# Sixteen dense tokens moved to the row path of a PEER layer, the V pass turned feature-major, and the last norm of the dense tokens with it

## The reference, cut to what matters

```python
q = (xt @ w_pq).reshape(T, PEER_HEADS, PEER_QUERY)
s1 = einsum('thd,nd->thn', q[..., :PEER_HALF], sub_keys1)
s2 = einsum('thd,nd->thn', q[..., PEER_HALF:], sub_keys2)
...                                   # top 16 of each, top 16 of their 256 sums
gate = softmax(top_s)                 # idx: (T, 8, 16) numbers of experts
u_sel = take(peer_u, ib, axis=0)
act = gelu(einsum('thkd,td->thk', u_sel, xb)) * gb
v_sel = take(peer_v, ib, axis=0)
out = einsum('thk,thkd->td', act, v_sel)
x = layer_norm(DN_ALPHA * x + out, ln3_g, ln3_b)
```

## Time and profile before

| | |
|---|---|
| median of 3 runs | 3217.24 us (3212.23 to 3222.93) |
| the profiled execution's own time | 3216.38 us |
| its span, first to last instruction | 3214.6 us |
| TensorE busy | 3086.2 us, 96% |
| VectorE busy | 2062.2 us, 64% |
| GpSimd / ScalarE busy | 656.9 us, 20% / 362.9 us, 11% |
| moved by DMA | 1029.74 MB, mean 320 GB/s |
| granted TensorE clock, mean | 0.986 |

### The profile page before, as it was taken

How to read it: one execution, slowest core, us unless ns; L and a number is a source line. 1 busy time by engine, 2 the same in 40 slices (tenths; PEclk the granted TensorE clock), 3 DMA queues, 4 the chain that set the end, 5 groups by cost and what they waited for, 6 DMA issues and landing times.

```text
span 3214.6 us, 26896 instructions
## 1 busy us (share of the span) xinstructions
PE 3086.2 (96%) x10342; PEld 1887.6 (59%) x10342; DVE 2062.2 (64%) x3070; ACT 362.9 (11%) x650; POOL 656.9 (20%) x551
## 2 busy tenths in 40 slices
PE   8999999999998998899988999999999999999797
PEld 5444444444446676679863447885448874478543
DVE  5365533433767788979996866655566565656684
ACT  1223212301002111112210000000000000000000
POOL 0000000000221133331223342222222222222340
PEclk9999999999999999999999999999999999999999
DMA  7222221077995699999989999999999999999994
GB/s 274 73 78 72 83 77 47 36 275 245 377 422 231 272 367 377 380 383 354 382 336 414 376 419 421 422 418 416 418 421 422 419 418 416 421 421 421 413 411 185
DMA packets 152520, 1029.74 MB, mean 320 GB/s; under 512 B 16464, under 2 KB 21712, under 8 KB 35664
## 3 DMA queue, kind: packets, MB, share of 16 engines
q0 software_dynamic: 78512, 557.88, 42.4%
q1 hardware_dynamic: 73888, 470.24, 37.5%
HBM read 1007.08 MB, written 20.97 MB: 320 GB/s over the span
## 4 chain that ended last, share of the span: by engine, by line
DMA 42%; PE 33%; DVE 19%; issue 4%; POOL 1%; ACT 1%; DVEq 0%; SPq 0%; ACTq 0%
DMA arena<-peer_v,arena 39%; PE ps L707 11%; DVE arena L1880 7%; PE ps L1143 5%; PE ps L1116 3%; PE ps L879 2%; PE ps L897 2%; DVE arena L1921 2%; DVE arena L1869 2%; PE ps L778 1%; DVE arena L1918 1%; DMA arena<-peer_ut 1%; DVE arena L1807 1%; PE ps L671 1%; PE ps L832 1%
## 5 line engine op out<-in xcount | busy, mean ns | idle before, releaser
L1143 PE MATMUL ps<-arena 128*128 128x512 f32 x2048 | 887.6, 596 | 38.7 <-DVE arena L1932 35.2
L1116 PE MATMUL ps<-arena 128*128 128x256 f32 x4096 | 893.9, 380 | 5.2 <-DMA arena<-peer_ut 4.6
L1116 PEld LDWEIGHTS ps<-arena 128*128 128x128 f32 x4096 | 776.2, 190 | 113.2 <-DMA arena<-peer_ut 5.7
L1880 DVE SCALAR_TENSOR_TENSOR arena<-arena 128x2048 f32<-128x2048 f32 x256 | 601.5, 2349 | 305.3 <-DMA arena<-peer_v,arena 234.7
L1869 DVE CUSTOM_DVE_ANT_0 arena<-arena 128x2048 f32<-128x2048 f32 x256 | 585.9, 2289 | 288.1 <-DMA arena<-peer_u,arena 287.2
L1143 PEld LDWEIGHTS ps<-arena 128*128 128x128 f32 x2048 | 391.4, 191 | 532.6 <-issue 488.6
L628 POOL DMA_INDIRECT arena<-peer_u,arena x256 | 326.8, 1277 | 1085.3 <-DVE arena L1869 909.1
L639 POOL DMA_INDIRECT arena<-peer_v,arena x256 | 307.9, 1203 | 756.6 <-DVE arena L1880 731.4
L707 PE MATMUL ps<-arena 128*128 128x512 f32 x800 | 345.2, 592 | 1.0 <-ACT arena L1183 1.0
L707 PEld LDWEIGHTS ps<-arena 128*128 128x128 f32 x800 | 152.0, 190 | 191.9 <-issue 191.9
L1183 ACT ACTIVATE arena<-ps 128x512 f32<-128x512 f32 (+2 forms) x247 | 144.2, 613 | 726.1 <-PE ps L889 136.7
(11 more groups left out here) (181 smaller groups left out, 1791.3 us busy)
## 6 DMA issues: line engine op xcount, KB each, us to landing
arena<-peer_ut SPq DMA_DIRECT2D x128, 1024.0 KB, 9.2
arena<-peer_vt SPq DMA_DIRECT2D x128, 1024.0 KB, 9.1
arena<-w_row SPq DMA_DIRECT2D x52, 1024.0 KB, 8.9
arena<-w_mix SPq DMA_DIRECT2D x48, 1024.0 KB, 5.8
arena<-w_once SPq DMA_DIRECT2D x74, 512.0 KB, 3.5
arena<-w_feat SPq DMA_DIRECT2D x20, 1024.0 KB, 9.6
dense_gates<-arena SPq DMA_DIRECT2D x8, 2048.0 KB, 8.5
arena<-dense_gates POOLq DMA_DIRECT2D x11, 1024.0 KB, 24.2
```

The costliest lines, as they stand in the source:

```text
L1116: last = pe.matmul(ps[:, (e // 2) % 4, (e % 2) * DT:(e % 2 + 1) * DT], w[:, kt * P:(kt + 1) * P], XTD[:, kt * DT:(kt + 1) * DT], start=(kt ...
L1143: last = pe.matmul(bank(4 + (c % 2) * 2 + tb), G[:, t * DT + tb * P:t * DT + (tb + 1) * P], w[:, i * 512:(i + 1) * 512], start=(t == 0), s ...
L1880: dve.scalar_tensor_tensor(out=acc, in0=VB[e], scalar=AV[r // 4 % 2][:, r % 4:r % 4 + 1], in1=acc, op0=ALU.mult, op1=ALU.add).then_inc(v_f ...
```

## The change

The first 240 of the 256 dense tokens stay dense (`DN` = 240). The last 16 (`NX`) go to the row path as a third set of rows: 16 tokens x 8 heads fill the 128 partitions, so 16 rows r are enough for them, against 128 for a full block (`QUADS` = 68 quads where there were 64). They stand at quads 60 to 63 (`XQUAD` = 60); the last four quads of block 1 move behind them. Their x is written to DRAM once per head and read back as one tile `XE` (over `SC`), their expert numbers and gates go the same way; ScalarE starts the accumulator `ACCE` at alpha x / 8, and at the end TensorE sums the eight heads with a stationary 128x16 matrix `SEL`.

U tiles now move 240 columns where they moved 256. In the V pass `peer_vt` is stationary (128 experts x 128 features) and `G` moves, 240 tokens; a tile is 16 matmuls; the output is feature-major in `YT`. There are eight column groups c of 256 features (`NC`), and c = 0 and 1 alternate tile by tile, so that each weigh still stands ahead of two tiles. The gates are made for 60 fours of tokens, stored in ten groups of 24. The statistics of the last norm of the dense tokens come from TensorE with a matrix of ones (`sums`), the norm is done on feature-major tiles by VectorE and ScalarE, and the host turns the output. The two gain tiles of the last norm are loaded later.

```diff
-ET = 4
+ET = 8
+NC = 8
+NX = 16
+DN = DT - NX
-TG = 32
+TG = 24
+NQ = DN // 4
+QUADS = RSTEPS + TOPK // 4
 def half_pos(k):
     n = k - HALVES_BEFORE
-    return 1 + n if n < 4 else 5 + (n - 4) * (POSITIONS - 8) // (2 * RSTEPS - HALVES_BEFORE - 4)
+    return 1 + n if n < 4 else 5 + (n - 4) * (POSITIONS - 8) // (2 * QUADS - HALVES_BEFORE - 4)
+XROWS_POS = POSITIONS - 2 * TILES[3] + 6
+XQUAD = min(j for j in range(QUADS) if half_pos(2 * j - 2) >= XROWS_POS)
+def v_order(g):
+    last = TILES[g] // ET
+    return [(c, l) for l in range(last) for c in (0, 1)] + [(c, l) for c in range(2, NC) for l in range(last)]
...
+            def store_extra():
+                sp.wait_ge(steps_dv, DVE_AT["d.x2_1"])
+                for h in range(PH):
+                    sp.dma_start(rows_d[:, h, :], X[P - NX:P, 3 * D:4 * D]).then_inc(extra_out, 16)
+                sp.wait_ge(extra_set, 1)
+                sp.dma_start(idx_d, S1D[P - NX:P, HK:2 * HK].bitcast(I32)).then_inc(extra_out, 16)
+                sp.wait_ge(gated, 12)
+                sp.dma_start(gate_d, GATE4[P - NX:P, 3 * HK:4 * HK]).then_inc(extra_out, 16)
...
+                if p == u3 + SLOTS:
+                    c, l = v_order(2)[-1]
+                    sp.wait_ge(wb_used, W_AT[f"V2.{c}.{l}"])
+                    sp.dma_start(XE, rows_d.rearrange("t h n -> (t h) n")).then_inc(xe_in, 16)
+                if p == u3 + TILES[3] + SLOTS + 6:
+                    sp.wait_ge(g_ready, NK // 8)
+                    sp.dma_start(GAIN3_G, gains[6:7, :].partition_broadcast(P)).then_inc(gain3_in, 16)
+                    sp.dma_start(GAIN3_B, gains[7:8, :].partition_broadcast(P)).then_inc(gain3_in, 16)
...
-                    last = pe.matmul(ps[:, (e // 2) % 4, (e % 2) * DT:(e % 2 + 1) * DT], w[:, kt * P:(kt + 1) * P],
-                                     XTD[:, kt * DT:(kt + 1) * DT], start=(kt == 0), stop=(kt == KT - 1))
+                    last = pe.matmul(ps[:, (e // 2) % 4, (e % 2) * DT:(e % 2) * DT + DN], w[:, kt * P:(kt + 1) * P],
+                                     XTD[:, kt * DT:kt * DT + DN], start=(kt == 0), stop=(kt == KT - 1))
...
-                    for i in range(4):
-                        t = 4 * l + i
-                        last = pe.matmul(bank(4 + (c % 2) * 2 + tb), G[:, t * DT + tb * P:t * DT + (tb + 1) * P],
-                                         w[:, i * 512:(i + 1) * 512], start=(t == 0), stop=(t == TILES[g] - 1))
+                for i in range(ET):
+                    t = ET * l + i
+                    for k in range(2):
+                        last = pe.matmul(ps[:, 4 + (c % 2) * 2 + k, 0:DN], w[:, (2 * i + k) * P:(2 * i + k + 1) * P],
+                                         G[:, t * DN:(t + 1) * DN], start=(t == 0), stop=(t == TILES[g] - 1))
+            def sums(c):
+                pe.wait_ge(sq_ready, c + 1)
+                for k in range(2):
+                    f = 2 * c + k
+                    pe.matmul(ps[:, 0, 0:DN], ONES, YT[:, f * DN:(f + 1) * DN], start=(f == 0), stop=(f == KT - 1))
+                    last = pe.matmul(ps[:, 1, 0:DN], ONES, SQ3[c % 2][:, k * DN:(k + 1) * DN],
+                                     start=(f == 0), stop=(f == KT - 1))
+                last.then_inc(sums_mm, 1)
+            def extra_heads(half):
...
+                for k in range(2):
+                    q = 2 * half + k
+                    pe.matmul(ps[0:NX, 2 + k, :], SEL, ACCE[:, q * 512:(q + 1) * 512], start=True, stop=True
+                              ).then_inc(extra_mm, 1)
...
             def dot(r):
-                b = r // HK
-                dve.tensor_tensor_reduce(UB[e], UB[e], xrow(b), 1.0, 0.0, ALU.mult, ALU.add,
+                if r == 4 * XQUAD:
+                    dve.wait_ge(xe_in, 16)
+                xr = XE if is_extra(r // 4) else xrow(main_quad(r // 4) // (HK // 4))
+                dve.tensor_tensor_reduce(UB[e], UB[e], xr, 1.0, 0.0, ALU.mult, ALU.add,
...
+                    if g == 3 and (c, l) == (6, 0):
+                        dve.wait_ge(extra_ev, 4)
+                        norm(XE, XE, GAIN3_G, GAIN3_B, dve_tick).then_inc(y_ready, 1)
...
+            dve.wait_ge(sums_mm, NC)
+            link(dve.tensor_scalar(MU3, ps[:, 0, 0:DN], 1.0 / D, None, ALU.mult))
...
+            rsqrt(RSTD3, VAR3, NEWTON3)
+            for k in QUAD:
+                ys = tile_rows(YT, 4 * k, 4)
+                link(dve.tensor_tensor(ys, ys, MU3.unsqueeze(1).broadcast_to([P, 4, DN]), ALU.subtract))
+                dve.tensor_tensor(ys, ys, RSTD3.unsqueeze(1).broadcast_to([P, 4, DN]), ALU.mult).then_inc(scaled, 1)
```

More of the change, by code:

```diff
@@ L147, in weigh_pos @@
     return start + 12 + 8 * i if 8 * i + 8 < TILES[g] else start + TILES[g]
-GATES_AFTER = {q: 2 * sum(1 for k in range(2 * RSTEPS) if half_pos(k) < weigh_pos(q - 2)) + 5 for q in range(5, NK // 8)}
+GATES_AFTER = {q: 2 * sum(1 for k in range(2 * QUADS) if half_pos(k) < weigh_pos(q - 2)) + 5 for q in range(5, NK // 8)}
 def pairs_of(unit):
@@ L319, in build @@
         GAIN1_G, GAIN1_B = place("gain1 g", D, SC2), place("gain1 b", D)
-        GAIN3_G, GAIN3_B = place("gain3 g", D, SC), place("gain3 b", D)
+        XE, ACCE = place("rows of extra tokens", D, SC), place("acc of extra tokens", D)
+        assert 32768 + TILES[3] * DN <= SC
         DPR, DPRT = place("dense probs", 2048, SC2), place("dense probs T", 2048)
@@ L380, in feature, with tile_rows @@
             return Y4[:, :, bass.ds(kt, 1), :].rearrange("p b a t -> p b (a t)")
+        def tile_rows(v, first, count):
+            return v.rearrange("p (k t) -> p k t", k=KT)[:, first:first + count, 0:DN]
         def by_block(v):
@@ L548, in beside @@
                     load_gates(4)
[L549 to L555, removed]
+                u3 = 2 * sum(TILES[:3])
+                if p == u3 + SLOTS:
[6 more added lines that the diff above has]
+                    sp.dma_start(GAIN3_B, gains[7:8, :].partition_broadcast(P)).then_inc(gain3_in, 16)
             p = 0
@@ L565, in _ @@
                     p += 1
[L566 to L570, removed]
+                for c, l in v_order(g):
+                    pair(peer_vt[(FIRST[g] // ET + l) * NC + c], f"V{g}.{c}.{l}")
+                    beside(p)
+                    p += 1
             sp.wait_ge(y_ready, 1)
@@ L1168, in _ @@
             for g in range(4):
-                for c in QUAD:
-                    for l in range(TILES[g] // ET):
-                        v_quad(g, c, l)
+                for c, l in v_order(g):
+                    v_unit(g, c, l)
+                    if g == 3 and c > 0 and l == TILES[g] // ET - 1:
+                        sums(c - 1)
+                        if c in (3, 4):
+                            extra_heads(c - 3)
                 if g < 3:
@@ L1537, in rows_until @@
             def rows_until(p):
-                while steps[0] < RSTEPS and half_pos(2 * steps[0] - 1) <= p:
+                while steps[0] < QUADS and half_pos(2 * steps[0] - 1) <= p:
                     gelu_rows()
@@ L1553, in _ @@
                         p += 1
-            rows_until(POSITIONS)
-            assert order == ACT_STEPS and steps[0] == RSTEPS
+            act.wait_ge(extra_in, 48)
+            for k in QUAD:
+                act.wait_ge(scaled, k + 1)
+                for f in range(4 * k, 4 * k + 4):
+                    yt = YT[:, f * DN:(f + 1) * DN]
+                    act.activation(yt, yt, ACT.Identity, scale=G3C[:, f:f + 1], bias=G3C[:, KT + f:KT + f + 1]
+                                   ).then_inc(yt_ready, 1)
+            assert order == ACT_STEPS and steps[0] == QUADS
         @block.vector
@@ L2041, in rows_until @@
             def rows_until(p):
-                while rows[0] < 4 * RSTEPS and half_pos(rows[0] // 2) <= p:
+                while rows[0] < 4 * QUADS and half_pos(rows[0] // 2) <= p:
                     some_rows(2)
@@ L2051, in rows_until @@
                     gates(12 + ROUTE_POS[p - 3], 1, ROUTE_POS[p - 3])
[L2053 to L2057 removed]
             p = 0
             for g in range(4):
[L2061 to L2063 removed]
+                for c, l in v_order(g):
+                    if g == 3 and (c, l) == (4, 0):
                         dve.wait_ge(gain3_in, 32)
```

263 lines of the change are left out of this document (159 added, 104 removed).

## The result

The change takes 3328.22 us (median of four runs, 3325.61 to 3330.71) against 3216.60 us (four runs of before): ratio 1.034, 95% interval 1.033 to 1.035. 3295 was forecast, with 3262 to 3325 as the range; the time lies 3 us above it. Direction and main cause came out as forecast, the size did not. The profiled execution of the change took 3330.71 us, 2.5 above the median.

The account below looks back on a forecast made before the run. VectorE's row stream, limited by DMA at about 421 GB/s, was taken to bound the kernel up to the last weigh. Span 3214.6 + 64 + 8 + 6 = 3292.6 us, forecast as 3295 us execution time, range 3262 to 3325.

Parts of the forecast that it names:

- The main step: Up to the last weigh: 14 more rows, 28 gathers, net +27.4 MB, cost +65 us at 421 GB/s.
- The start of V0, forecast -6: Before the first weigh: fewer one-hots save VectorE 7 us, new operations give back 0.7; -6 us, between -10 and +8.
- The ten stores instead of eight are each smaller: Start of V0: ScalarE's staging tile, which held VectorE up once for 10.5 us, may do so more or less.
- The stretch to the last weigh, +70 forecast: First to last weigh: +65 us for added bytes and +5 for a lower mean rate.
- I take +5: Up to the last weigh: +5 us for a lower mean DMA rate from bursty tiles, few row buffers and smaller gate pieces.
- ends in waiting: Up to the last weigh: TensorE's 77 us saving over 192 tiles is hidden by VectorE's lateness.
- V3, +8 forecast: Last weigh to last addition: TensorE's faster tiles plus new sums take 147 us against 139.1, +8.
- Both fit under 147: After the last weigh: VectorE's 121 us and DMA's 102 us fit beside TensorE's 147; if not, +10.
- The last norm, +6 forecast: After the last tile: final norm and store take 25.5 us against 19.4, +6, between +3 and +11.
- TensorE stays the bound: Rival for the whole kernel: DMA carries more than 421 GB/s, TensorE's saving shows, 3128 us; 4 in 100.
- The bytes find room: Rival in U0 and early V0: spare DMA room takes the 27 MB, only the ends count, 3223 us; 4 in 100.
- TensorE gets slow by waiting: Rival in V0 to U3: waits lower TensorE's clock, decisive under 0.85; at 0.82, 3353 us; 5 in 100.

Follow-up runs that it names:

- experiment 1: Two runs of the change: without the 16 extra rows, 3256.60 us; with the gathers for the extra tokens half as wide, 3287.41 us.
- experiment 2: The change with U tiles of 256 columns as before: 3331.52 us, ratio 1.0356 to the kernel before.
- experiment 3: The change with SP's ten small stores moved, eight singly ahead of the one-hot stage, two behind the first gate stores: 3319.46 us.
- experiment 4: The change with the U pass's PSUM banks lent to c = 2 and 3 of V0 to V2: 3319.36 us, ratio 1.0306.
- experiment 5: The change with the sums over squares in V3 one column group later: 3326.88 us, ratio 1.0335.
- experiment 7: The change with stores spread, new banks in V0 to V2, later sums, and other banks for c = 2 to 7 of V3: 3303.20 us.
- experiment 8: As experiment 7, but without the extra rows: 3227.22 us, ratio 1.0032 to the kernel before.

## Why the prediction was wrong in size

**The main step held.** "28 gathers ... +27.4 MB ... +65 us": 28 gathers and 25.7 MB came, and taking the rows out gave 68 us on that stretch, half their bytes 40 (experiment 1). That DMA's 421 GB/s is the limit and that TensorE's saving is hidden also held: records of 240 columns come every 201 ns, TensorE is busy for 90% where "about 87%" was said, and U tiles as wide as before cost nothing (experiment 2).

**The start of V0, forecast -6, came +11.** The step that failed is "The ten stores instead of eight are each smaller; ScalarE's staging tile held VectorE up once ... it may do so more or less". The stores of gates did not do it. The ten small stores ahead of them on SP's queue did, and the prediction never priced them, although the change names them: 12 us of issue, passed on through ScalarE. With them spread (experiment 3), 9 us of the time come back, and the first weigh starts at 1660 to 1668 us in the four profiled kernels that have this edit, around the forecast's 1662; in those without it, at 1674 to 1683. The means of the two sets lie 15 us apart; with a scatter of 8 or 9 us in either, that accounts for the 17. That 1662 was met to the microsecond in experiment 3 is luck.

**The stretch to the last weigh, +70 forecast, +77 measured.** The term that was mis-sized is "I take +5" for a lower mean rate. The 25.7 MB make 61 us at 421 GB/s; the other 16 are the rate, 598 MB at 409 GB/s where it was 414. The prediction reckoned with 419 before the change for the whole piece, but that was the stage behind 1900 us alone. Nearly all of the 16 is the hole in V0: 360 instead of 387 GB/s over 219 us are 5.9 MB, 14 us at 421. The prediction said that TensorE's saving "ends in waiting", and took any place for the waits as free. The one that ended at 1794 was not, as both users of DMA stood still. New banks for V0 to V2 gave 9 us back (experiment 4).

**V3, +8 forecast, +20 measured.** The step that failed is "Both fit under 147". It compared totals, VectorE's 121 and DMA's 102 us against TensorE's 147, and not the order within: the addition of c = 0 stands behind the rows of five positions, which are four rows, 18.6 us of VectorE's work and some 6 of waiting, nearly all for gathers; TensorE is there after two tiles. The stop is 11.0 us and the lower clock behind it 2.6, more than the 12 that are missing. Moving the sums did nothing (experiment 5). Moving the banks took the stop away from c = 2, and 6.6 us came back at c = 3, since VectorE, which waits for gathers, is late too (experiment 7). Only with the new banks and without the extra rows does V3 run through, TensorE's part from 3050.82 to 3195.41, 145 us (experiment 8): the forecast had the price of TensorE's work right and its freedom from stops wrong.

**The last norm, +6 forecast, +5.5 measured.**

**The range.** 3325 as the upper end was too low by the prediction's own terms. The start is given as -6 with -10 to +8 as its bounds, so it could come out 14 above; the sum of the bounds takes it as 8. Those 6 us more would have put the range's end at 3331 and the measured 3328 inside it. That would have been width and not insight, since the stores and the stops would still have been missing.

**The rivals.** "TensorE stays the bound": no window goes above 423 GB/s. "The bytes find room": they did not. "TensorE gets slow by waiting": its clock fell to 0.88 in V0 and to 0.95 from 1900 us to the last weigh. From 1780 to 1800 us it was 0.50, which is the lower of the two levels, 1.2 GHz; TensorE had stopped at 1763 and went on at 1794. The forecast put the point where it would decide under 0.85, and over V0 to U3 it was 0.94. Before the last weigh experiment 2 makes it likely that the clock costs nothing; in V3 it cost the 2.6 us above.

**The signs.** Of those named for "right", the rate and the records came. VectorE did not wait "for gathers alone": 10.6 us were for TensorE. The last weigh came at 3142 where "near 3118" was said.

## What to carry to other kernels

Where a streaming engine is 98% busy and DMA runs at its ceiling, ask which of them the other waits for before trading one for the other: 6% fewer columns in the U pass bought nothing, and 28 gathers, 29 MB, ahead of the last weigh cost some 70 us. A written order has to be followed at every place where one engine catches up with another, since a sum that fits over a stage can still stop the engine at its head; and a stop costs most where the other user of the resource is busy elsewhere, as in V0 here. What is late can often be put behind the point that waits: four rows and two tiles moved behind the last weigh are worth 14 to 18 us.

## What was not expected of the hardware

Eight DMAs of 16 partitions in a row took SP 9.00 us to issue, 1.1 us each, and the two that follow 1.5 and 1.4; the single DMAs of all 128 partitions around them took 0.32 to 0.64. Issued singly in experiment 3, 4 to 8 us apart with a tile between, each of the eight took 0.42 to 0.69:

```profile
1409.59 0.43 SPq L578 DMA_DIRECT2D extra_rows<-arena  x1
```
